# Clearing a stage's semaphores in runs, and loading the first weight tile ahead of the token tiles in two projection stages

## The reference

```python
for layer in range(2):
    h = _rms(x, pre_norm[layer])
    m = _even_mixer(h, ...) if layer % 2 == 0 else _odd_mixer(h, ...)
    x = x + _rms(m, post_norm[layer])
```

## Time and profile before

| | |
|---|---|
| median of 3 runs (lowest, highest) | 3583.0 us (3576.31, 3585.24) |
| profiled execution, own time | 3579.12 us |
| its span | 3577.5 us, 45195 instructions |
| busy PE / PEld / DVE / ACT / POOL | 96% / 79% / 46% / 40% / 19% |
| mean granted TensorE clock | 0.978 of full speed |
| stage `ef`, `gl`, `at`, `eo` begin at about | 0, 733, 903, 1473 us |
| stage `of`, `mh`, `oo` begin at about | 1750, 2917, 3298 us |

### The profile page before, as it was taken

One profiled execution on the slowest core, in us unless ns is written; L12 is line 12 of the kernel. 1 busy time (PEld: TensorE's weight loads), 2 busy tenths in 40 slices (PEclk: granted clock), 3 DMA queues, 4 the chain that ended last, 5 costly groups with the idle time before them and its releaser, 6 DMA issues. The chain is left out here.

```text
span 3577.5 us, 45195 instructions
## 1 busy us (share of the span) xinstructions
PE 3417.9 (96%) x16886; PEld 2816.4 (79%) x16886; DVE 1659.9 (46%) x3061; ACT 1424.4 (40%) x2491; POOL 687.5 (19%) x493
## 2 busy tenths in 40 slices
PE   7999999979799999899799999999999989997998
PEld 5788788857688888788687878788788878886887
DVE  4899999526555555511303232232323415555311
ACT  4233332143266666500224545445553234553200
POOL 4121221111201110033221011111112113331231
PEclk8999999999899999999899999999999999998999
DMA  4333332276421211633323232322322543333531
GB/s 123 88 86 93 97 96 84 78 218 200 148 57 40 55 43 40 172 106 94 104 84 101 84 117 74 118 66 88 105 82 81 207 151 95 113 95 112 171 97 62
DMA packets 436743, 368.83 MB, mean 103 GB/s; under 512 B 73720, under 2 KB 373112, under 8 KB 436528
## 3 DMA queue, kind: packets, MB, share of 16 engines
q1 hardware_dynamic: 351088, 271.55, 26.3%
q10 hardware_dynamic: 85440, 94.39, 7.5%
HBM read 238.11 MB, written 127.75 MB: 102 GB/s over the span
## 5 line engine op out<-in xcount | busy, mean ns | idle before, releaser
L2723 PE MATMUL of_ring<-of_hhi,of_whi 128*128 128x512 f32 x1368 | 552.1, 404 | 1.9 <-issue 1.0
L2725 PE MATMUL of_ring<-of_hhi,of_wlo 128*128 128x512 f32 x1368 | 535.9, 392 | 0.0
L2724 PE MATMUL of_ring<-of_hlo,of_whi 128*128 128x512 f32 x1368 | 534.1, 390 | 0.0
L2296 POOL TENSOR_TENSOR of_wlo<-of_wraw,of_whi 128x1024 fp32r<-128x1024 f32 x57 | 143.9, 2525 | 931.6 <-ACT of_whi L2329 931.6
L2723 PEld LDWEIGHTS of_ring<-of_hhi,of_whi 128*128 128x128 f32 x1368 | 257.8, 188 | 67.6 <-issue 15.2
L781 PE MATMUL ef_ring<-ef_hhi,ef_whi 128*128 128x512 f32 x744 | 298.9, 402 | 3.6 <-POOL ef_hlo L340 2.4
L2725 PEld LDWEIGHTS of_ring<-of_hhi,of_wlo 128*128 128x128 f32 x1368 | 257.3, 188 | 55.8
L2375 ACT ACTIVATE of_stage<-of_ring 128x512 f32<-128x512 f32 x219 | 127.0, 595 | 432.9 <-PE of_ring L2725 432.3
L2724 PEld LDWEIGHTS of_ring<-of_hlo,of_whi 128*128 128x128 f32 x1368 | 258.3, 189 | 49.4
L783 PE MATMUL ef_ring<-ef_hhi,ef_wlo 128*128 128x512 f32 x744 | 291.5, 392 | 0.0
L782 PE MATMUL ef_ring<-ef_hlo,ef_whi 128*128 128x512 f32 x744 | 290.8, 391 | 0.0
(11 more groups left out here) (439 smaller groups left out, 7636.5 us busy)
## 6 DMA issues: line engine op xcount, KB each, us to landing
of_wraw<-o_w_in SPq DMA_DIRECT2D x56, 512.0 KB, 3.8
ef_wraw<-e_w_in SPq DMA_DIRECT2D x29, 512.0 KB, 4.2
s_tmo<-of_stage ACTq DMA_DIRECT2D x48, 256.0 KB, 2.3
s_uc<-ef_stage ACTq DMA_DIRECT2D x24, 256.0 KB, 2.6
ef_ut<-s_uc SPq DMA_DIRECT2D x16, 384.0 KB, 4.1
s_za<-ef_stage ACTq DMA_DIRECT2D x24, 256.0 KB, 2.4
s_gt<-ef_stage ACTq DMA_DIRECT2D x32, 192.0 KB, 2.9
s_zb<-ef_stage ACTq DMA_DIRECT2D x24, 256.0 KB, 2.2
```

Of the source, the lines that this page charges most:

```text
L2296: pool.tensor_tensor(wlo[k % 2][:, :, :], wraw[:, :, :], whi[k % 2][:, :, :].bitcast(F32), ALU.subtract).then_inc(wlo_done, 1)
L2723: pe.matmul(out, ah, hhi[:, f, tc], start=(f == 0), stop=False)
L2724: pe.matmul(out, ah, hlo[:, f, tc], start=False, stop=False)
L2725: mm = pe.matmul(out, al, hhi[:, f, tc], start=False, stop=(f == KT - 1))
```

## The change

`Stage.__exit__` sorts the stage's semaphore numbers, joins neighbouring numbers into runs, and clears each run with one instruction. In both front stages weight tile 0 is loaded first, its high part is ScalarE's first work and its low part VectorE's instead of GpSimd's; weight tile 1 is loaded behind tile 5, and its high part moves from ScalarE's round 5 to round 6. In `ef` GpSimd also sets a small tile `warm`, and ScalarE takes a square root of it ahead of everything, which adds two semaphores.

```diff
     def __exit__(self, *a):
-        for x in self.sems:
-            self.nc.tensor.sem_clear(x)
+        for a, n in self.runs():
+            self.nc.tensor.sem_clear(range(a, a + n))
         self.ctx.close()
+    def runs(self):
+        out = []
+        for n in sorted(x.num for x in self.sems):
+            if out and n == sum(out[-1]):
+                out[-1][1] += 1
+            else:
+                out.append([n, 1])
+        return out
...
# SyncE, ef (of: the same with NT for 8)
+                w_load(0)
                 x_load(0)
                 sp.dma_start(ident[:, :], d["ident"][:, :]).then_inc(const_in, 16)
                 sp.dma_start(gcol[:, :], d["pre_col"][0]).then_inc(const_in, 16)
-                for i in range(1, 4):
-                    x_load(i)
-                w_load(0)
-                for i in range(4, 7):
+                for i in range(1, 6):
                     x_load(i)
                 w_load(1)
-                x_load(7)
+                for i in range(6, 8):
+                    x_load(i)
...
# GpSimd (the memset in ef only)
+                pool.memset(warm[:, :], 1.0).then_inc(warm_set, 1)
                 for i in range(NT):
-                    if i == 1:
-                        w_lo(0)
                     if i == 5:
                         w_lo(1)
...
# ScalarE (the first two lines in ef only)
+                act.wait_ge(warm_set, 1)
+                act.activation(warm[:, 1:2], warm[:, 0:1], ACT.Sqrt).then_inc(warm_done, 1)
+                w_hi(0)
                 act.wait_ge(const_in, 32)
                 square(0)
...
-                    if i in (1, 5):
-                        w_hi(i // 5)
+                    if i == 6:
+                        w_hi(1)
...
# VectorE, ef (of: the same without the regrouping of columns)
+                dve.wait_ge(whi_done, 1)
+                tt(grouped(wlo[0][:, :, :]), by_group(wraw[:, :, :]), grouped(whi[0][:, :, :]).bitcast(F32), ALU.subtract).then_inc(wlo_done, 1)
                 dve.wait_ge(const_in, 32)
                 mean(0)
```

More of the change, by code:

```diff
@@ L161, in even_front @@
         ss = [s.sb(f"ss{u}", [P, 4]) for u in range(4)]
+        warm = s.sb("warm", [P, 2])
         keep = s.sb("keep", [P, Q])
@@ L204, in even_front @@
         pb = [tq[:, 0:512], tq[:, 512:1024]]
-        const_in, s5_in = s.sem("const_in"), s.sem("s5_in")
+        const_in, s5_in, warm_set, warm_done = (s.sem(x) for x in ("const_in", "s5_in", "warm_set", "warm_done"))
         x_in = [s.sem(f"x_in{u}") for u in range(4)]
@@ L2248, in _ @@
                 sp.dma_start(gcol[:, :], d["pre_col"][1]).then_inc(const_in, 16)
[L2249 to L2252, removed]
+                for i in range(1, 6):
                     x_load(i)
                 w_load(1)
-                for i in range(7, NT):
+                for i in range(6, NT):
                     x_load(i)
@@ L2617, in root_mean @@
                     dve.reciprocal(w_[:, 3:4], w_[:, 2:3]).then_inc(ors_done, 1)
+                dve.wait_ge(whi_done, 1)
+                tt(wlo[0][:, :, :], wraw[:, :, :], whi[0][:, :, :].bitcast(F32), ALU.subtract).then_inc(wlo_done, 1)
                 dve.wait_ge(const_in, 32)
```

## The result

The changed kernel takes 3556.25 us (median of 4 runs, 3554.31 to 3556.61) against 3581.97 for the kernel before (4 runs, 3576.31 to 3585.24): a ratio of 0.9929 with a 95% interval of 0.9912 to 0.9946, so 25.7 us faster, 19 to 32 by the interval. The profiled execution took 3556.5 (span 3554.9) for 3579.1 before, 22.6 us less.

What follows compares the result with a forecast made beforehand. TensorE, busy 96% of the span, was taken as the bound, so only its standing time could be won. Clears 8.7, front of `ef` 5.4 and of `of` 0.6 sum to 14.7 us; forecast 3567, range 3559 to 3577.

Steps and rivals of the forecast that it cites:

- `eo`, 3.6 forecast: Start of `eo`: with joined clears the first matmul moves from 1479.16 to about 1475.5, when its operands are ready; 3.6 us.
- `oo`, 2.1 forecast: Start of `oo`: with joined clears the first matmul moves from 3303.15 to about 3301.0; 2.1 us.
- rival D: Start of `eo`: shorter idleness keeps TensorE's clock high, so the first 9 matmuls gain 1.8 us more; 3565, chance 0.08.
- The end 2.5: End of the kernel: the last 25 clears, about 3.0 us, become 4 runs of 0.5 us; gain 2.5 us.
- `mh` 0.5: Clears of `mh`: its 79 clears end at 2926.5, the operand that counts was ready at 2925.93; gain 0.5 us.
- The price of a run: All joined clears: clearing a run should cost about what one clear costs, 0.12 us.
- Rivals B: Joined clears: a run costs 0.12 us a member, so only the fronts gain, 6.0 us; 3576, chance 0.08.
- C: Joined clears: a run costs over 0.12 us a member, kernel slower from 0.15; 3592 at 0.2, chance 0.04.
- `gl`, 0 forecast: Clears of `gl`: an earlier start is eaten by the 5.1 us wait for the second weight tile's low part; 0.
- Front of `ef`: Start of `ef`: a walk through each engine's order puts group 0 at 29.0 for 33.83; 5.4 us with the clock's 0.6.
- Rival A: Both fronts: tiles come 2 us late and the fronts give nothing, leaving the clears' 8.7 us; 3573, chance 0.18.
- Front of `of`: Start of `of`: first square 1.9 us later, group 0 0.9 us earlier, less 0.3 for the low clock; 0.6 us.

Runs made afterwards that it cites:

- e1_clears_only: The kernel before with only the clears joined into runs, both front stages as before: 3564.55 us, ratio 0.9956.
- e12_single_after_at: The changed kernel, but the 53 semaphores of stage `at` cleared one by one: 3562.20 us, ratio 0.9949 against the kernel before.
- e2_fronts_only: The changed kernel with all clears single again, both front stages as changed: 3570.42 us, ratio 0.9971 against the kernel before.
- e4_of_front: The kernel before with only the front of `of` changed, clears single: 3575.44 us, ratio 0.9985.
- e6_without_of_front: The changed kernel with the old front of `of`: 3560.79 us, ratio 0.9945 against the kernel before.
- e8_tile0_first: The changed kernel with tile 0 and constants loaded ahead of the weights in both fronts, splits one place later: 3557.66 us, ratio 0.9937 against the kernel before.

## Why the prediction was off, step by step

**`eo`, 3.6 forecast, 6.4 measured, and `oo`, 2.1 forecast, 3.8 measured: the step that failed.** The prediction says "the first operands are ready when VectorE's second low part ends". They are ready before the stage begins. The kernel before splits item 0's weights and its tokens (an item is one block of rows of the output weights, with its tokens) a stage ahead: `ahead.high(act, 0)` and `ahead.low(dve, 0)` stand at lines 1547 and 1655, inside `at`, and at 3159 and 3262, inside `mh`. The timeline of the kernel before has their low parts, the last operands to be made, over 10 us ahead of the barrier of 1472.61 and 34 us ahead of that of 3298.07:
```profile
1460.08 1.22 DVE L1817 TENSOR_TENSOR ew_wlo<-ew_raw,ew_whi 128x1024 fp32r<-128x1024 f32 x1 [1.79 <-ACT ew_whi L1810]
1461.22 0.55 DVE L1819 TENSOR_TENSOR ew_ylo<-ew_xt,ew_yhi 128x384 fp32r<-128x384 f32 x1
...
3261.91 1.23 DVE L1817 TENSOR_TENSOR ow_wlo<-ow_raw,ow_whi 128x1024 fp32r<-128x1024 f32 x1 [1.52 <-ACT ow_whi L1810]
3263.05 0.55 DVE L1819 TENSOR_TENSOR ow_ylo<-ow_xt,ow_yhi 128x384 fp32r<-128x384 f32 x1
```
The first split behind the barrier is item 1's. The row was there to see it: the earlier trace rows has VectorE writing `eo_wlo`, and the matmul of 1479.16 reading `ew_whi` and `ew_yhi`. I went by order of time, and for `oo` by the chain of waits, which had stepped to a split that ended next to the wait. What TensorE waited for at both places was its own clears. The whole block is won: the first matmul of `eo` moves from 6.56 to 0.81 behind the barrier, 5.75 us, that of `oo` from 5.08 to 0.62, 4.46. `e1_clears_only` shows it for both places by making the joined clears the only edit, and `e12_single_after_at` for `eo` by taking the joining away at this barrier alone. That the later operands come in time was right: in the traces of the changed kernel and of `e1_clears_only` TensorE doesn't stand again in the first 60 us of either stage.

**The clock at these places.** The granted clock by windows of the changed kernel (window; its length, busy us of PE, PEld, DVE, ACT, POOL; PEclk, DMA share, GB/s):
```profile
1461.00:1462.00 1.00, 0.80 (x4) 0.70 (x5) 0.49 (x1) 0.90 (x2) 0.00 (x0) 1.00 0.39 94
1462.00:1463.00 1.00, 1.00 (x5) 0.79 (x4) 1.00 (x2) 0.00 (x0) 0.00 (x0) 0.69 0.81 266
1463.00:1464.00 1.00, 1.00 (x4) 0.81 (x3) 0.21 (x1) 0.00 (x0) 0.00 (x0) 0.50 0.99 236
...
1466.00:1468.00 2.00, 2.00 (x11) 1.60 (x10) 1.69 (x2) 0.63 (x3) 0.00 (x0) 1.00 1.04 248
...
3283.00:3288.00 5.00, 5.00 (x13) 3.85 (x13) 2.89 (x4) 1.92 (x4) 0.00 (x0) 0.50 0.92 327
```
After 3.45 us without work TensorE enters `eo` at 1.00 of 2.4 GHz, falls to 0.50 within 2 us, although it doesn't pause, and is back at 1.00 by 1466. Before it entered after 9.4 us at 0.50. The high level at the entry isn't what makes `eo` win 0.6 us more than its start: of the eight traces with joined clears there, five enter at the high level and three don't (`e1_clears_only` at 0.58 in its first microsecond), and all eight stages take 271.5 to 271.6. What they share is that only 7 or 8 of the first 24 matmuls go at the low rate (0.43 us from one to the next for 0.23), and 10 or 11 in the five traces with single clears (13 where they are doubled). From the first to the 24th it takes 6.9 us for 7.5 in the mean, and this is the 0.6. So of rival D's 1.8 us a third came, and not by its reason, a high level that stays. `oo` enters at 0.50 after 6.4 to 7.3 us; over nine traces 9 to 13 of its first 24 go at the low rate, 13 in this one, for 7 or 8 in four before. That is 0.7 us lost in the mean, so its stage wins 3.8 where its start moved by 4.46. Why the low stretch is shorter in the one place and longer in the other isn't tested.

**The end 2.5, measured 2.4; `mh` 0.5, measured 0.3.** Right. The number of clears was right too (10 to 16, 13 came).

**The price of a run.** The prediction took 0.12 us flat and kept a price for each member as the alternative. It is in between: some 0.5 us for 60. The Trainium skill (Runtime: NRT & Kernel Launch, The launch sequence) gives some 1.5 us for a reset of 51 semaphores per engine, an estimate of 29 ns for each; the run of 60 takes 8 ns each, and the measurement decides. Rivals B (0.12 us a member) and C (more than 0.15) are out: 60 members would take 7.2 us or more and took 0.485.

**`gl`, 0 forecast, 1.4 measured.** The step was right as far as it went: TensorE starts 1.6 us sooner (5.46 behind the barrier for 7.07), and the wait for the second weight tile ends 47.0 us behind the barrier for 47.6, in the mean of nine traces 47.5 for 47.4 in four unchanged ones: the gain is eaten there, as forecast. But a later wait was left out of the sum. The kernel before stands once more, in the list of its waits:
```profile
PE gl_acc L1127 <- ACT gl_sq L1039: 3.8, 1, 3.8
```
It is 1.5 in the changed kernel (line 1142), 2.6 to 3.8 in the four traces with single clears and 1.4 to 2.3 in the nine with joined ones, and ends 1.0 us earlier in the mean. What makes ScalarE's `gl_sq` earlier isn't tested, and 1.4 is half of what single traces stray.

**Front of `ef`, 5.4 forecast, 6.0 measured.** The walk holds at nearly each station: weights landed at 5.17 (5.0 forecast), `w_hi(0)` to 7.1 (7.0), the low part 1.90 with regrouped columns (1.22 to 2.3), `root(0)` at 10.95 (11.2), `h_hi(0)` at 15.6 (16.0), group 0 at 28.09 (29.0). That the flip would be last was wrong: the flip ended at 27.74 for 28.9, and GpSimd at 27.94, and GpSimd is last by 0.2 to 0.4 us in all seven traces with this front. In them group 0 begins at 28.1 to 29.6, 5.0 us earlier in the mean for the 4.8 of the walk. In this pair of traces 9 of its matmuls went at the low rate for 13 before, and group 1 came 6.5 us earlier where group 0 came 5.7: 0.8 for the 0.6 that I had set for it. Over all traces the numbers overlap, 6 to 12 for 7 to 13, and the mean is 0.4; that the shorter gap ahead of the group is the cause isn't shown. Rival A (the fronts give nothing) is out by `e2_fronts_only`.

**Front of `of`, 0.6 forecast, 1.5 by the stages.** Group 0 was forecast 26 us behind the barrier for 26.9 and came at 25.1 to 26.5 in six traces, for 26.9 to 28.4 in the four with the old front: 1.8 us earlier in the mean where 0.9 was forecast. The first square comes 5.85 behind the barrier for 3.9, the 1.9 later that was forecast; the first flip is only 1.3 later. The 0.3 that I took off for the low clock had the wrong sign: the group's 24 matmuls took 0.6 us less in the mean, with a wide scatter. The mechanism stands, its size was 1 us off. By times its gain is larger, 5.3 in `e4_of_front` and 4.5 in `e6_without_of_front`. What makes up the other 3 us stays open: the traces of these kernels don't show it, the interval of the first reaches down to 2.1, and the second isn't apart from the changed kernel by its interval.

**The sum.** 21.8 by the stages for 14.7: 2.8 of the 7.1 missing are `eo`'s, 1.7 `oo`'s, 1.4 `gl`'s, 0.9 `of`'s and 0.6 `ef`'s, and 0.3 are taken off by `mh` and the end. Another 4 us between the stages and the medians are within the interval of the ratio and aren't explained. The lower end of the range was also 1 us too high for its own terms, a gain of 21 from 3579 being 3558; the measured 3556.25 lies below either.

## What to carry to other kernels

When a wait is put down to "issue", look at what the waiting instruction reads, by buffer name, and find who wrote that. The operation that ends beside the wait may belong to the next item. Clears in an engine's sequencer at the head of a stage cost their full time where the operands were made ahead; one or two range clears in their place moved the first matmul 5.8 us forward for 53 semaphores and 4.5 for 41. In a front, follow each queue to the first instruction that releases another engine, and ask what stands ahead of that one: in `e8_tile0_first` the first square came 2.1 us earlier, and the first that releases somebody 1.5 us later.

## What the runs showed of the hardware

- A range clear of 60 semaphores takes 485 ns, of 41 357 ns; single clears of 56 ns come 0.12 us apart, so 41 of them take 5 us.
- After 3.45 us of idleness TensorE's granted clock was 1.00 at the first matmul of the changed kernel's `eo` and 0.50 two us later, under unbroken work; in `e1_clears_only`, after 3.46 us, it was 0.58 in the first microsecond and then 0.50. At the other entries of `eo` and `oo`, after 6.4 to 15.8 us of idleness, the first matmuls came 0.43 us apart or more, the low rate, in every trace.
- A VectorE subtraction of 128x1024 took 1.90 us with regrouped columns (`ef`) and 1.22 without (`of`).
- Stages whose code is the same differed by 3 us and more from trace to trace (`at` 568.5 to 572.1), more than most of the terms of this sum.
